# A two-layer hybrid decoder trunk: first layer's tokens loaded as four half tiles, latents by tile and pass, rotary work behind the latents' norm

## The reference, cut to what matters

```python
h = rms_norm(x, attn_norm[i])
proj = h @ w_in[i]
...
mla = proj[..., OFF_MLA:OFF_MLA + MLA_COLS]            # 192 + 128 + 32 = 352 columns
c_q = rms_norm(mla[..., :MLA_Q_RANK], mla_q_norm[i])
c_kv = rms_norm(mla[..., MLA_Q_RANK:MLA_Q_RANK + MLA_KV_RANK], mla_kv_norm[i])
k_pe = mla[..., MLA_Q_RANK + MLA_KV_RANK:]
q_m = (c_q @ mla_w_uq[i]).reshape(B, S, H, MLA_QK)
kv_m = (c_kv @ mla_w_ukv[i]).reshape(B, S, H, MLA_NOPE + MLA_V)
...
q_m = jnp.concatenate([q_m[..., :MLA_NOPE], rope(q_m[..., MLA_NOPE:], positions)], axis=-1)
```

## Time and profile before

| | us |
|---|---|
| median of 3 timed runs | 658.26 |
| their lowest and highest | 658.02, 658.28 |
| the profiled execution | 658.76 |
| its span in the trace | 656.9 |

### The profile page before, as it was taken

One profiled execution on the slowest core, in us unless ns is written; L12 is line 12 of the kernel. 1 busy time (PEld: TensorE's weight loads), 2 busy tenths in 40 slices (PEclk: granted clock), 3 DMA queues, 4 the chain that ended last, 5 costly groups with the idle time before them and its releaser, 6 DMA issues.

```text
span 656.9 us, 9644 instructions
## 1 busy us (share of the span) xinstructions
PE 648.3 (99%) x3774; PEld 558.8 (85%) x3774; DVE 507.4 (77%) x729; ACT 432.2 (66%) x649; POOL 329.4 (50%) x196
## 2 busy tenths in 40 slices
PE   8999999999999999999999999999999999999997
PEld 6988887888888888888889879878888888888885
DVE  5997778749878768996488777886699778789933
ACT  6669886676766674654474789856776766664632
POOL 5443500288888885006841353004888888820091
PEclk9999999999999999999999999999999999999999
DMA  9972125675555555653387431165555555555411
GB/s 320 372 252 65 65 101 160 198 247 192 189 187 191 185 189 191 212 196 108 109 287 248 154 102 65 66 196 189 193 192 193 191 189 189 188 194 204 161 32 65
DMA packets 74606, 115.38 MB, mean 176 GB/s; under 512 B 2368, under 2 KB 58432, under 8 KB 74304
## 3 DMA queue, kind: packets, MB, share of 16 engines
q1 hardware_dynamic: 73408, 111.95, 51.0%
q10 hardware_dynamic: 1152, 2.81, 1.2%
HBM read 113.70 MB, written 1.05 MB: 175 GB/s over the span
## 4 chain that ended last, share of the span: by engine, by line
PE 94%; DVE 3%; DMA 1%; ACT 1%; issue 0%; POOL 0%; SPq 0%; DVEq 0%; ACTq 0%; POOLq 0%
PE ps L1580 24%; PE ps L1027 14%; PE ps L1029 14%; PE ps L1028 14%; PE ps L1582 12%; PE ps L1173 1%; PE ps L1079 1%; DMA raw<-w_in 1%; PE ps L1199 1%; PE ps L1439 1%; PE ps L1041 1%; PE ps L1114 1%; PE ps L1211 1%; DVE hn L2286 1%; PE ps L1640 1%; PE ps L1642 1%
## 5 line engine op out<-in xcount | busy, mean ns | idle before, releaser
L496 POOL TENSOR_TENSOR wl<-raw,wh 128x2048 fp32r<-128x2048 f32 (+1 forms) x58 | 259.0, 4468 | 155.9 <-DVE x L2275 90.5
L1580 PE MATMUL ps<-hT_hl,wh 128*128 128x512 f32 x688 | 238.6, 392 | 0.0
L627 ACT ACTIVATE wh<-raw 128x2048 fp32r<-128x2048 f32 (+1 forms) x100 | 180.5, 1808 | 49.9 <-DVE raw L2216 23.6
L1582 PE MATMUL ps<-hT_hl,wl 128*128 128x256 f32 x688 | 193.3, 281 | 0.0
L1580 PEld LDWEIGHTS ps<-hT_hl,wh 128*128 128x128 f32 x688 | 129.1, 188 | 28.2
L1582 PEld LDWEIGHTS ps<-hT_hl,wl 128*128 128x128 f32 x688 | 129.4, 188 | 0.0
L1027 PE MATMUL ps<-wh,hT_hl 128*128 128x512 f32 (+1 forms) x216 | 79.7, 369 | 0.0
L1029 PE MATMUL ps<-wh,hT_hl 128*128 128x512 f32 (+1 forms) x216 | 77.4, 358 | 0.0
L1028 PE MATMUL ps<-wl,hT_hl 128*128 128x512 f32 (+1 forms) x216 | 77.4, 358 | 0.0
L483 POOL TENSOR_SCALAR st<-st 128x2 f32<-128x2 f32 (+3 forms) x22 | 6.5, 294 | 114.0 <-ACT lat L702 62.2
L2175 DVE SCALAR_TENSOR_TENSOR pb<-ps,conv,pb 128x255 f32<-128x255 f32 (+1 forms) x96 | 39.5, 472 | 17.3 <-ACT pb L918 17.3
(11 more groups left out here) (362 smaller groups left out, 1281.5 us busy)
## 6 DMA issues: line engine op xcount, KB each, us to landing
raw<-w_up SPq DMA_DIRECT2D x44, 1024.0 KB, 5.1
raw<-w_down SPq DMA_DIRECT2D x22, 1024.0 KB, 4.9
raw<-w_in SPq DMA_DIRECT2D x16, 1024.0 KB, 9.7
raw<-w_o SPq DMA_DIRECT2D x6, 1024.0 KB, 4.9
raw<-ple_gate SPq DMA_DIRECT2D x6, 1024.0 KB, 4.8
raw<-w_in SPq DMA_DIRECT2D x4, 704.0 KB, 5.2
ng<-norm_gains ACTq DMA_DIRECT2D x2, 1024.0 KB, 6.7
raw<-w_o SPq DMA_DIRECT2D x4, 512.0 KB, 4.0
```

The lines of the kernel that those rows point to most:

```text
L496: pool.tensor_tensor(wl[:, slot, 0:n], raw[:, slot, 0:n], w_high(u)[:, 0:n].bitcast(F32), ALU.subtract).then_inc(done, 1)
L627: act.activation(w_high(u)[:, c:n], raw[:, slot, c:n], ACT.Copy).then_inc(h_made, 1)
L1580: pe.matmul(both, high[:, c], hU_all[:, k].rearrange("p a n -> p (a n)"), start=k == 0, stop=False, skip_group_check=True)
L1582: mm = pe.matmul(o, wl[:, slot, c], hU_h[:, k, :], start=False, stop=k == KT - 1, skip_group_check=True)
```

## The change

It touches the first layer alone. SP loads x as four quarters in the order 0, 2, 1, 3 (`FIRST`: first the left halves of both tiles, then the right ones), and between the two pairs the latents' first weights in two pieces of two row blocks. All that counts quarters in the first layer goes through `turn`, which gives a quarter's place in that order. TensorE turns quarters 0 and 2, multiplies tile 0 with unit 0, turns 1 and 3, multiplies tile 1 with unit 0; unit 1 is then multiplied tile by tile in three passes over its four row blocks (high with high, high with rest, rest with high). ACT and DVE treat quarters in the same order. The rotary steps move: the angles' first five steps behind `low(M_SB_Q)`, the other seven (`rope_remainders`) behind the latents' sums, together with the wide roots; the sines on ACT behind the copies of the turned latents; and the tables (`rope_tables`, with `rope_done`) and the shared key's rotation behind `sb_rooted`, ahead of `low(5)`.

```diff
+FIRST = (0, 2, 1, 3)
+def turn(layer, n, k):
+    return FIRST.index(k) if layer == 0 and n == 0 else k
...
-            for t in range(TT):
-                sp.dma_start(x[:, t, :], x_in[0, t * P:(t + 1) * P, :]).then_inc(x_landed[t], 16)
+            def load_x(k):
+                t, c = quarter(k)
+                sp.dma_start(x[:, t, c], x_in[0, t * P:(t + 1) * P, c]).then_inc(x_landed[k], 16)
+            for k in FIRST[0:2]:
+                load_x(k)
...
                 for u, (c, w, k, n) in enumerate(WIN_PARTS):
+                    if layer == 0 and u == M_MLA_A:
+                        sp.dma_start(raw[:, u, 0:2 * w].rearrange("p (k n) -> p k n", k=2),
+                                     rows(w_in, 0, 2)[:, :, c:c + w]).then_inc(first_rows, 16)
+                        sp.dma_start(raw[:, u, 2 * w:4 * w].rearrange("p (k n) -> p k n", k=2),
+                                     rows(w_in, 2, 2)[:, :, c:c + w]).then_inc(raw_landed[u], 16)
+                        for q in FIRST[2:4]:
+                            load_x(q)
+                        continue
...
-                    for t in range(TT):
-                        act.wait_ge(x_landed[t], 16)
-                        for half in range(2):
-                            x_square(2 * t + half).then_inc(F["x_squared"], 1)
+                    for k in FIRST[0:2]:
+                        act.wait_ge(x_landed[k], 16)
+                        x_square(k).then_inc(F["x_squared"], 1)
                     act.dma_start(pos_i[:], positions).then_inc(pos_landed, 16)
-                    x_high(0, AT_START)
+                    x_high(0, AT_START, FIRST[0:2])
+                    for k in FIRST[2:4]:
+                        act.wait_ge(x_landed[k], 16)
+                        x_square(k).then_inc(F["x_squared"], 1)
                     latent_high(pt_r, M_MLA_B, 0, "mla_high")
+                    x_high(0, AT_START, FIRST[2:4])
...
                 if layer == 0:
-                    x_T(x, AT_START, None)
-                    project_tile(M_MLA_A, 0, (0, 1), 0, quarters=0)
-                    project_tile(M_MLA_A, 1, (0, 1), 0, quarters=0)
+                    x_T(x, AT_START, None, quarters=FIRST[0:2])
+                    pe.wait_ge(first_rows, 16)
+                    latent_A_plain(0, range(0, 2))
+                    pe.wait_ge(raw_landed[M_MLA_A], 16)
+                    latent_A_plain(0, range(2, 4))
+                    x_T(x, AT_START, None, quarters=FIRST[2:4])
+                    latent_A_plain(1, range(4)).then_inc(w_used, 1)
                     for t in range(TT):
-                        latent_B(t, False)
-                        latent_B(t, True)
+                        latent_B_by_pass(t)
...
                 if layer == 0:
                     dve.wait_ge(gcol_landed, 16)
-                    for k in range(4):
+                    for k in FIRST[0:2]:
                         turned(layer, k)
-                    x_low(0, AT_START)
+                    x_low(0, AT_START, FIRST[0:2])
+                    for k in FIRST[2:4]:
+                        turned(layer, k)
                     latent_low(wl[:, M_MLA_B], pt_r, M_MLA_B, 1, "mla_high", "mla_low")
+                    x_low(0, AT_START, FIRST[2:4])
...
-                if layer == 0:
-                    rope_angles()
                 low(M_SB_Q, halves=True)
...
+                if layer:
+                    roots_wide()
+                else:
+                    rope_angles()
-                if layer == 0:
-                    rope_tables()
                 low(3)
...
                 sums_made(last, 1)
+                if layer == 0:
+                    roots_wide()
+                    rope_remainders()
...
                 sb_rooted(slice(0, P), slice(H, H + 2), 3, 1.0)
+                if layer == 0:
+                    rope_tables()
+                    key_rotation()
                 low(5)
```

More of the change, by code:

```diff
@@ L347, in build @@
         w_used = sem("w_used")
-        x_landed = [sem(f"x_landed{t}") for t in range(TT)]
+        x_landed = [sem(f"x_landed{k}") for k in range(4)]
+        first_rows = sem("first_rows")
         pos_landed = sem("pos_landed")
@@ L735, in _ @@
                         act.activation(o[:], t[:], ACT.Copy).then_inc(signs_made, 1)
-                if layer == 0:
-                    act.wait_ge(rope_arg, 1)
-                    for table, a in ((rope_s[:, :, 32:64], 0), (rope_c[:, :, 0:32], 64)):
-                        act.activation(table, tmp[:, a:a + 64].rearrange("p (t n) -> p t n", t=TT),
-                                       ACT.Sin).then_inc(rope_sin, 1)
                 act.dma_start(pT[:], p_cols[layer]).then_inc(F["p_landed"], 16)
@@ L762, in _ @@
                            "lat_T", 1 + t, "cT_ready")
+                if layer == 0:
+                    act.wait_ge(rope_arg, 1)
+                    for table, a in ((rope_s[:, :, 32:64], 0), (rope_c[:, :, 0:32], 64)):
+                        act.activation(table, tmp[:, a:a + 64].rearrange("p (t n) -> p t n", t=TT),
+                                       ACT.Sin).then_inc(rope_sin, 1)
                 high(5)
@@ L1959, in _, with roots_wide @@
                         x_low(0, AT_START, (k,))
-                if layer == 0:
-                    rope_angles()
-                low(M_SB_Q, halves=True)
-                dve.wait_ge(F["roots"], base["roots"] + 2)
-                for t in range(TT):
-                    last = ts(tmp[:, 768 + t * P:768 + (t + 1) * P], neg_ones[:],
-                              stat(ST_X + 6 + t), -1.0, ALU.mult, ALU.mult)
-                last.then_inc(F["roots_wide"], 1)
-                if layer == 0:
-                    rope_tables()
+                low(M_SB_Q, halves=True)
+                def roots_wide():
+                    dve.wait_ge(F["roots"], base["roots"] + 2)
+                    for t in range(TT):
+                        last = ts(tmp[:, 768 + t * P:768 + (t + 1) * P], neg_ones[:],
+                                  stat(ST_X + 6 + t), -1.0, ALU.mult, ALU.mult)
+                    last.then_inc(F["roots_wide"], 1)
+                if layer:
+                    roots_wide()
+                else:
+                    rope_angles()
                 low(3)
@@ L1998, in _, with key_rotation @@
                            .broadcast_to([P, TT, PE_DIM]), ALU.mult))
-                chained(rope32(kpe[:], kp, [tmp[:, 576 + 64 * a:640 + 64 * a].rearrange(
-                    "p (t n) -> p t n", t=TT) for a in range(2)], [P, TT]))
+                def key_rotation():
+                    chained(rope32(kpe[:], kp, [tmp[:, 576 + 64 * a:640 + 64 * a].rearrange(
+                        "p (t n) -> p t n", t=TT) for a in range(2)], [P, TT]))
+                if layer:
+                    key_rotation()
                 dve.wait_ge(F["roots"], base["roots"] + 3)
```

30 lines of the change are left out of this document (25 added, 5 removed).

## The result

| | before | after |
|---|---|---|
| median of the 7 timed runs of each | 658.26 | 660.12 |
| lowest and highest | 658.02, 659.00 | 659.41, 661.71 |
| the profiled execution, its span | 658.76, 656.9 | 660.07, 658.3 |

What follows compares the result with a forecast made beforehand. TensorE, busy 99%, was taken to bound the kernel. A gain of 0.5 us at the latents' norm, already counted in a net 1.6 us lateness at M_MOBA_B, gave 658.26 + 1.6 = 659.9; range 658.6 to 661.1.

Steps and rivals of the forecast that it cites:

- Tables ahead of the root: POOL's tables, queued ahead of the key root, delay it to 44.4 and low(6) to 48.35; M_MOBA_B starts 1.6 us later.
- the rivals' own test: At the key root on POOL: if it came by about 42.4, TensorE would not wait and the tables had slipped through.
- (a): Rival: POOL's tables end by 39.5, the root is not late, and the time is 657.8; chance 0.15.
- (b): Rival: DVE holds POOL's tables at every step, +2.6 us, 660.9; a fall of TensorE's clock belongs here; chance 0.07.
- One term: On DVE ahead of the sums over heads: table steps 0.77, key rotation 0.69, low(5) from 35.4 to 37.7; by itself hidden.
- The start: Up to M_SB_Q: quarters and weights in pieces let TensorE start M_SB_Q at 16.1 and not 16.83, a gain of 0.7.
- I cost the issues at nothing: SP's three more DMAs ahead of unit 1 cost nothing, as DMA held a backlog; if some came late, some 0.3 us.
- The norm: The latents' norm on DVE begins at 23.9 and not 24.39, so all behind it is 0.5 us earlier.
- the sum: At M_MOBA_B: start at 48.4 against 46.76, 1.6 us later, with the 0.5 won at the norm already in it.
- 658.26 + 1.6: The forecast time: the kernel before's median plus the 1.6 us of lateness at M_MOBA_B, giving 659.9.
- (c): Rival: more issues and packets put off all landings, M_SB_K's among them, by 0.5 to 1; 660.4 to 660.9; chance 0.03.
- the fall of the clock: Part of rival (b), chance 0.07: TensorE's clock falls through the idle 2 us; granted clock 1.00 in every stretch spoke against it.

Runs made afterwards that it cites:

- The two runs that take the wait away by different edits: The changed kernel with POOL's tables behind the roots of keys and queries: 659.22; the changed kernel with low(6) ahead of DVE's wait for the key root: 659.14.
- the half tiles alone: The kernel before, with x loaded as four half tiles in the order 0, 1, 2, 3 ahead of the weights, nothing else changed: 659.21, ratio 1.0014.
- `low(6)` first: The changed kernel, with DVE making low(6) ahead of its wait for the key root in the first layer: 659.14, ratio 1.0010.
- the kernel of all but the start: The kernel before, with the rotary and wide-root moves, POOL's tables behind the roots and low(6) ahead of DVE's wait; start unchanged: 657.28, ratio 0.9983.
- the order alone: The kernel before, with only the start's order of work on ACT, DVE and TensorE changed; loads and rotary work as before: 662.17, ratio 1.0052.
- the old loads: The changed kernel, with x loaded as two whole tiles and unit 0 in one piece, as in the kernel before: 659.64, ratio 1.0026.

## Why the prediction was right, and where it was not

- **Tables ahead of the root: right, in mechanism and size.** Forecast and measured: `rope_done` 34.7 and 34.9; `low(5)` done 37.7 and 38.65; tables done 42.1 and 42.0; the root 44.4 and 44.3; `low(6)` done 48.35 and 48.3; `M_MOBA_B` 48.4 and 48.34. One table product was held by `low(5)` and one by line 2135, as counted. By the rivals' own test the tables did not slip through (a), and were not held at every step (b): beside the two sums over heads they ran at 0.46 and 0.3 each. The two runs that take the wait away by different edits show it by its removal: 0.9 and 1.0 us in the medians. One term was too small, and the root did not depend on it: DVE's own steps beside POOL's tables got longer (the rotation took 1.2 us and not 0.69, `low(5)` 2.46 and not 2.28, line 2135 1.19 and not 0.96), so DVE was about 1 us late itself and idled 1.54 for the root and not 2.7.
- **The start: wrong.** The step that failed is "`M_SB_Q` starts at 16.1 and not 16.83, a gain of 0.7". It came at 17.9. I let the landing of unit 1 (12.74) bound the gain and took TensorE to be free by then; but the right halves' transposes, which ran free in the wait for the weights, were put on TensorE's path (0.87), and "I cost the issues at nothing" was wrong by 1.8 us in unit 1's landing (the half tiles alone: 1.0). Its ground, "350 to 390 GB/s throughout", holds for rows from 13.9 us on (and one of them has 338); none is of the stretch in which x lands. What the new start costs shows in the runs that leave the root's wait out: 0.8 to 0.9 us over before in the medians, with the norm's gain of 0.95 already in them, and 659.14 (`low(6)` first) against 657.28 in the kernel of all but the start, which differs from it in the start and in the place of POOL's tables.
- **The norm: the place right, the size wrong, twice.** `M_SB_K` did not come at 16.3 but after 17.3, so the norm began at 24.86 and not 23.9. But TensorE was 1.1 late by then, and did not wait. And what the late norm had cost was 0.95 and not 0.5.
- **Why the sum came out all the same.** TensorE came to `M_MOBA_B` at 46.8 and not 46.3, which only made its wait 1.6 and not 2.1; the start there is set by POOL and DVE, whose times the forecast had right. Where a later wait sets the time, an error ahead of it is swallowed. The late start thus cost next to nothing in this sum, and reappears in the medians when the wait is taken away. Part of the good number is luck: 658.26 + 1.6 takes the difference at `M_MOBA_B` for that of the medians. In the profiled executions it was 1.58 there and 1.3 at the end, and the medians differ by 1.86; what the other half us is, no row shows.
- **DVE caught up.** It was 0.96 late at the norm against forecast and 0.2 late at the tables (34.14 against 33.9): with POOL's tables gone from beside them, a pair of the norm's steps took 0.62 and not 0.79. Whether that is all of the 0.7 won back was not measured apart.
- **The rivals.** (c), late pieces, had 0.03 and happened (unit 1 by 1.8), beside the forecast's mechanism and hidden by it; its chance was far too low. Of the fall of the clock I had said that a row after 1.29 us idle spoke against it. In the profiled execution of the changed kernel it did not fall (1.00 through the start and in the idle time at `M_MOBA_B`); it fell in two other orders, after eight transposes and 2.3 us idle.
- **What the Trainium skill said.** That `tensor_reduce` does not contend with GpSimd (the Trainium skill, SBUF — State Buffer, section "Who interferes with whom") had no row for or against it: now the trace agrees, as POOL's products took 0.46 at 39.07 and 0.60 for two at 39.48, beside both sums, and 2.65 for two beside `low(5)`.

What stays open: why the clock fell, and how often. Among the profiled executions with eight transposes ahead of unit 0, it fell after 2.33 and 2.36 us idle (the order alone, the old loads) and not after 0.33 to 1.43 (five others), but in one of the five (1.00 idle) the products were as slow as at half the clock though the record reads 1.00. With sixteen, and 0.99 to 1.39 idle, it stayed at 1.00 in five. The single executions warn against a rule: a mean clock of 0.997 or less, which goes with about 1 to 2 us more, stands in four of six of the order alone, two of six of the old loads and one of seven of the changed kernel, but also in two and three of eleven of the two kernels with x in quarters, which have sixteen transposes.

## What to carry to other kernels

Work that an engine does while it waits for a transfer is free only there: before starting on half the data, count what leaves the wait and falls on the path, on the waited engine and on those that must treat its output. When a product moves behind a slower producer, look not at who needs it but at what is queued behind the wait on each in-order engine; the cure may be one line, moving the queued instruction ahead (`low(6)`), or letting the short chain go first on POOL. And judge the parts apart: here one part was worth a 1.1 us gain with its order mended, and the whole change hid it.

## What the hardware did that I had not expected

- The granted clock of TensorE fell to 0.50 for 3.3 us after eight transposes and 2.3 us without work at the start, and cost 1.7 us; in the profiled executions with sixteen transposes and 1.0 to 1.4 us idle, and in the changed kernel's with eight and 1.43, it stayed at 1.00.
- Loads of x in rows of 2 KB moved 278 and 315 GB/s with the DMA engines as busy as at 354 GB/s with rows of 4 KB, from 2 to 5 us.
- A second queue for one 512 KB tile beside weights from SP made the tile later, and the weights hardly earlier: 0.6 us on the whole.
